# Places for the experts' weights: a ring of 15 in place of 5, and the blocks in another order

## The chip, the cores and the metric

The kernel runs on one core of one Trainium2 chip. The metric is the device time of one execution in microseconds (us). The kernel before took 3222.83 us as the median of three runs (3220.64 to 3227.54).

## What is computed

Three layers run one after the other over 512 tokens of 1024 features, all in float32. The change touches the mixture of experts in the second. There are 16 experts in 4 groups of 4; a token picks one group, and in it two experts:

```python
scores = jax.nn.sigmoid((t @ w_router).astype(jnp.float32))
sel = (scores + router_bias).reshape(-1, N_GROUPS, EXPERTS_PER_GROUP)
g_idx = jnp.argmax(lax.top_k(sel, TOP_K)[0].sum(-1), axis=-1)
in_group = jnp.take_along_axis(sel, g_idx[:, None, None], axis=1)[:, 0]
_, e_local = lax.top_k(in_group, TOP_K)
...
h = jax.nn.silu(jnp.einsum('td,edf->tef', t, w_gate)) * jnp.einsum('td,edf->tef', t, w_up)
y = jnp.einsum('tef,efd->td', h * combine[..., None], w_down)
```

Each expert's gate and up weights are 1024x256 and its down weights 256x1024. A layer norm (`ln1`) stands ahead of the experts, another (`ln2`) behind them.

## The kernel before

Each engine has its own program, written out by hand (`pe_experts`, `act_experts`, `dve_experts`, `pool_experts`), and they meet at semaphores. All weights lie in HBM as slabs of 128x1024 float32 (512 KB). SP, the queue of SyncE, loads them in order of use. The slab number n goes to place n % RING of a ring in SBUF, RING being 5, and its load waits until PE has used slab n - RING, which was there before it.

A float32 product is made of three products of rounded parts. For each slab, ACT copies a rounded high part to one of 3 buffers (`act_hi`), DVE subtracts it from the slab and writes the low part in place over the slab (`dve_lo`), and PE multiplies with both. ACT and DVE prepare slab i + 2 while PE uses slab i (`act_next`, `dve_next`: i + len(run.hi) - 1), since the high buffer of slab i + 3 is free only once PE is done with slab i.

**The experts.** The tokens are sorted into blocks of 128 rows: blocks 0 to 3 hold the first 128 tokens of groups 0 to 3, and three overflow blocks hold what is over 128 in any group. A block takes 24 slabs: 4 for the gate and up weights of each of its 4 experts (`up`), then 8 for the down weights (`down`). The seven blocks take 168 slabs, and go through in order: blocks 0 to 3 (96 slabs, loaded by SP), then the overflow blocks (72 slabs). Which group's weights an overflow block needs is known only from the router's result, so POOL loads those slabs with indirect DMAs (line 3488), whose row numbers lie in `m.place`. These too wait for slab n - RING.

In a block, PE does `up` for expert e, then `turn` (two transposes) for expert e - 1, and `rows` (8 small matmuls) once. The tokens of two blocks are brought to their rows at a time, by matmuls with one-hot matrices (`placed(g)`, 64 matmuls; `hot(g)` makes the matrices on DVE), ahead of `down` in blocks 1, 3 and 5. ACT and DVE copy the results to `m.xs`. Between the slabs ACT does the silu (`e_silu`) and copies the turned result (`e_Hhi`), and DVE does `gated` and `turned`. At a block's end ACT and DVE copy half of the output each (`m.ysb`), and ACT issues the store to `yd` (line 3298). At the very end POOL gathers each token's row from `yd` (line 3494).

`m.xs` and the one-hot matrices `m.hot` are each held twice, for the present pair of blocks and the next. In the last block DVE also adds 4 tiles of 128x1024 (`m.h`, the residual).

**Ahead of the experts** stands the stage `branches`. Its last slab on PE is used at 2344 us. ACT prepares the first experts' slabs in `act_first(K, m.we)`, as many as there are high buffers, ahead of `act_lnorm` for `ln1` (a table load, 8 squares, and the root); DVE takes two of them ahead of its last sum and the rest in `dve_first` behind its centring. PE sums the squares. Then come the router, transposes of the tokens (`x_trh`, `x_trl`), and `placed(0)`.

Line 410 is DVE's (and POOL's) tensor_tensor, line 403 ACT's copy, line 478 PE's matmul, line 482 its transpose.

```python
def act_hi(K, run, i):
    ...
    if i >= len(run.hi):
        A.wait_ge(*K.book.at("slab", run.name, i - len(run.hi)))
    elif run.behind:
        A.wait_ge(*K.book.at(*run.behind[i]))
    A.copy(run.hi[i % len(run.hi)][:, 0:run.offs[i][1]], raw, "hi", run.name, i)
```

Of the kernel before, what the change touches and what calls it, by code (L numbers as in the profile page):

```python
# [13 lines left out]
RING = 5  # L14
U32 = mybir.dt.uint32
SLAB = 1024
# [554 lines left out]


def landed(K, n):
    return K.book.at("slot%d" % (n % RING), n)


def raw_of(K, run, i):
    n = slab_at(K, "slab", run.name, i)
    size = run.offs[i][1]
    return n, K.ring[:, n % RING * SLAB:n % RING * SLAB + size], K.ring_r[n % RING][:, 0:size]  # L580

# [1468 lines left out]
def memory2(K, x):  # L2050
# [38 lines left out]
    m.xh = m.O[:, 0:8 * T]  # L2089
    m.xt, m.xs, m.hot, m.ysb = M(8 * T), M(16 * T), M(4 * T), [M(1024) for _ in range(2)]  # L2090
    m.xt_r, m.xl_r = M.rounded(m.xt, 1024), M.rounded(m.h, 1024)
# [3 lines left out]
    m.esg = [m.O[:, 8 * T + 256 * i:8 * T + 256 * i + 256] for i in range(4)]  # L2095
    wh = [M(1024), M(1024), m.O[:, 10 * T:12 * T]]
    m.x_r, m.xh_r = M.rounded(x, T), M.rounded(m.xh, T)
    m.we = Run(K, "experts", run_of(w0 + 89 * SLAB, 96) + [(None, SLAB)] * 72, wh, [("b_sum", 23)] * 3)
    m.wrh, m.wrl = M.rounded(M(256), 128)
# [5 lines left out]
    m.sw = [M(4) for _ in range(2)]  # L2105
    s = m.slot = M(292)
    m.slots = {"number": s[:, 0:256], "first": s[:, 256:272], "over": s[:, 272:288], "row": s[:, 288:289]}
# [1008 lines left out]

BLOCKS, PAIRS, EQ = 7, 4, ALU.is_equal


def pe_experts(K, m):  # L3120
# [39 lines left out]
    def placed(g):  # L3160

        P.wait_ge(*at("e_hot", g))
        P.wait_ge(*at("x_tl", 1, 3))
        for k in range(8):
            b = P.bank(1, "e_xs", g, k)
            for n, xt in enumerate((m.xt_r, m.xl_r)):
                for j in range(4):
                    P.mm(bk(b)[:, 256 * n:256 * n + 256], xt[j][:, 128 * k:128 * k + 128], m.hot_r[4 * (g % 2) + j][:], j == 0, j == 3)
            P.did("e_xsum", g, k)

    def rows(b):
        P.wait_ge(*at("r_w4"))
        o, S = P.bank(1, "e_rows", b), slice(128 * (b % 2), 128 * (b % 2) + 128)
        for n, w in enumerate((m.w4h, m.w4l)):
            for j in range(4):
                P.mm(bk(o)[:, 0:4], m.hot_r[4 * (b // 2 % 2) + j][:, S], w[:, 4 * j:4 * j + 4], n == 0 and j == 0, n == 1 and j == 3)
        P.did("e_rowed", b)

    def weights(i):
        n, raw = P.slab(m.we.offs[i][0], "slab", "experts", i)  # L3180
        P.wait_ge(*at("lo", "experts", i))
        return m.we.hi[i % 3], K.ring_r[n % RING]

    def up(b, e):
        o, lo = P.bank(1, "e_gated", b, e), 128 * (b % 2)
        for q in range(4):
            i = 24 * b + 4 * e + q
            wh, wl = weights(i)
            for h in range(2):
                k, C = 2 * q + h, slice(512 * h, 512 * h + 512)  # L3190
                xs = m.xs_r[8 * (b // 2 % 2) + k]
                P.wait_ge(*at("e_xs", b // 2, k))
                P.mm3([bk(o)], xs[:, lo:lo + 128], xs[:, 256 + lo:384 + lo], wh[:, C], wl[:, C], k == 0, k == 7)
            P.did("slab", "experts", i)
# [54 lines left out]
def act_experts(K, m, yd):  # L3249
# [16 lines left out]
    def placed(g, ks):  # L3266
        for k in ks:
            A.wait_ge(*at("e_xsum", g, k))
            A.copy(m.xs_r[8 * (g % 2) + k][:], out_of(K, 1, T, "e_xs", g, k), "e_xs", g, k)

# [5 lines left out]
    for b in range(BLOCKS):  # L3276
# [20 lines left out]
        A.wait_ge(*at("e_y", b, 1))  # L3297
        A.ready().dma_start(yd[128 * b:128 * b + 128, :], m.ysb[b % 2]).then_inc(*K.book.up("yst%d" % (b % 2), ("e_st", b), by=16))
    A.tables(ACT.Ln)
# [10 lines left out]
def dve_experts(K, m):  # L3310
# [14 lines left out]
    def hot(g):  # L3325
        for j in range(4):
            V.ts(m.hot_r[4 * (g % 2) + j][:], m.slots["number"], pos[:, j:j + 1], -256.0 * g, SUB, EQ, *(("e_hot", g) if j == 3 else ()))

# [11 lines left out]
    dve_shares(K, m)  # L3340
    hot(1)
    for b in range(BLOCKS):
        i = 24 * b
        for e in range(4):
            for q in range(4):
                dve_next(K, m.we, i)
                i += 1
            if e == 0:
                V.apart().wait_ge(*at("e_rowed", b))
                V.apart().cp(m.sw[b % 2], out_of(K, 1, 4, "e_rows", b), "e_rows", b)  # L3350
            gated(b, e)
            if e:
                turned(b, e - 1)
            if b == BLOCKS - 1:
                S = slice(1024 * e, 1024 * e + 1024)
                V.tt(m.h[:, S], m.xl_r[e][:], m.xt_r[e][:], ADD)
        if b % 2 and b // 2 + 1 < PAIRS:
            g = b // 2 + 1
            for k in range(1, 8, 2):
                V.wait_ge(*at("e_xsum", g, k))  # L3360
                V.cp(m.xs_r[8 * (g % 2) + k][:], out_of(K, 1, T, "e_xs", g, k), "e_xs", g, k)
            if g + 1 < PAIRS:
                hot(g + 1)
        for kk in range(8):
# [112 lines left out]
def pool_experts(K, m, table, wall, slots, yd):  # L3477
# [4 lines left out]
    G.wait_ge(*at("r_place"))  # L3482
    by_row = wall.rearrange("p (s c) -> (p s) c", c=SLAB)
    for n, (off, size, done) in enumerate(K.P.slabs):
        if off is None:
            slot = n % RING
            G.wait_ge(*at(*K.P.slabs[n - RING][2]))
            G.ready().indirect_dma_start(K.ring[:, slot * SLAB:slot * SLAB + SLAB], None, by_row,  # L3488
                                     bass.IndirectOffsetOnAxis(ap=m.place[:, 4 + (done[2] - 96) // 24:5 + (done[2] - 96) // 24], axis=0),
                                     element_offset=(done[2] - 96) % 24 * SLAB).then_inc(*K.book.up("gslot%d" % slot, ("slot%d" % slot, n), by=16))  # L3490
    for b in range(BLOCKS):
# [664 lines left out]
def layout_engines(nc, book, xT, out, con, par, wall, slots, at, blocks=(1, 2, 3)):  # L4156
# [11 lines left out]
    K.ring_r = K.mem.rounded(ring[:, :], SLAB)  # L4168
    half = K.mem.rounded(ring[:, :], HALF)
    K.halves = [half[2 * n:2 * n + 2] for n in range(RING)]  # L4170
    K.c, K.p = {}, {}
# [27 lines left out]
    with nc.Block() as block:  # L4199
# [63 lines left out]
        def _(eng):  # L4263
# [68 lines left out]
```

## Time and profile before

| | |
|---|---|
| median of 3 runs | 3222.83 us |
| the profiled execution's own time | 3222.16 us |
| its span, first to last instruction | 3220.1 us |
| PE busy | 2928.7 us (91%) |
| DVE busy | 1568.6 us (49%) |
| ACT busy | 1215.3 us (38%) |
| POOL busy | 826.5 us (26%) |
| moved by DMA | 283.09 MB, 88 GB/s over the span |
| issues of 512 KB by SP | 202, 3.7 us to landing |
| indirect DMAs of POOL | 72 |
| mean granted TensorE clock | 0.935 of full speed |

The page cuts the span into 40 slices of 80.5 us. Slices 31 to 34, from 2415 us to 2737 us, show 257, 275, 248 and 230 GB/s, where most others show 30 to 110. They lie within the experts' stage, and are the place to look at. The busy time of PE is modelled and takes in the overlap of matmuls, so the room on PE is better read from the starts of its weight loads (PEld).

### The profile page before, as it was taken

To read this page: it belongs to the slowest core of one execution; us is meant where nothing else is said; L and a number is where in the kernel's file an instruction comes from. 1 tells how busy PE (TensorE), PEld (TensorE's weight loads), DVE (VectorE), ACT (ScalarE), POOL (GpSimd) and SP (SyncE) were. 2 spreads that over 40 slices of the span, in tenths; PEclk is the share of its full clock that TensorE was granted. 3 is DMA by queue.
4 is the path that set the end of the run, shared out by engine and by line. 5 is a ranking of instruction groups with operands and counts; after the bars stand their busy time and mean duration, and the time that the engine had idled before them with its cause. 6 is when DMAs were issued, how large, how long until landed. Compare 5 with 4: busy or idle time off the path is not lost.

```text
span 3220.1 us, 54157 instructions
## 1 busy us (share of the span) xinstructions
PE 2928.7 (91%) x22694; PEld 2317.3 (72%) x22694; DVE 1568.6 (49%) x2880; ACT 1215.3 (38%) x2134; POOL 826.5 (26%) x814
## 2 busy tenths in 40 slices
PE   7899999999889999999899899998978887898998
PEld 6788888888767878887577677777756655556566
DVE  3544555455424344342443454566667766542433
ACT  2333333333322243232433344543255655442341
POOL 4222222222122100000345243541000055523243
PEclk9899899989889999999899898999999999878999
DMA  3111111111033333332122122224327877411112
GB/s 130 37 32 41 32 41 35 41 31 38 28 111 109 102 99 96 94 97 77 43 65 70 47 69 63 82 66 151 98 81 257 275 248 230 148 38 53 36 56 69
DMA packets 101266, 283.09 MB, mean 88 GB/s; under 512 B 11392, under 2 KB 11392, under 8 KB 99744
## 3 DMA queue, kind: packets, MB, share of 16 engines
q1 hardware_dynamic: 81968, 209.11, 21.5%
q0 software_dynamic: 14592, 60.56, 5.6%
q10 hardware_dynamic: 4464, 9.96, 0.8%
q8 instruction: 179, 2.93, 0.4%
q14 instruction: 63, 0.52, 0.1%
HBM read 261.24 MB, written 18.35 MB: 87 GB/s over the span
## 4 chain that ended last, share of the span: by engine, by line
PE 74%; DVE 10%; ACT 8%; DMA 5%; issue 2%; POOL 1%; ACTq 0%; DVEq 0%; SPq 0%; POOLq 0%
PE psum L478 72%; DVE arena L410 5%; ACT arena L395 4%; DMA ring<-in_w 3%; ACT arena L403 3%; DMA ring<-in_w,arena_whole 2%; PE psum L482 2%; DVE arena L419 2%; DVE ring L410 2%; ACT L390 1%; POOL ring L3488 1%; DVE arena L414 1%; DVE arena L422 1%; DVE arena L434 0%; DMA arena<-in_x 0%
## 5 line engine op out<-in xcount | busy, mean ns | idle before, releaser
L478 PE MATMUL psum<-arena,ring 128*128 128x512 f32 (+3 forms) x6152 | 1442.6, 365 | 13.5 <-DVE arena L410 6.9
L478 PEld LDWEIGHTS psum<-arena,ring 128*128 128x128 f32 (+2 forms) x6152 | 1024.4, 193 | 209.0 <-issue 35.6
L478 PE MATMUL psum<-arena 32*32 32x32 f32 (+16 forms) x12460 | 880.4, 254 | 154.2 <-DVE arena L410 58.4
L478 PE MATMUL psum<-arena,arena 128*128 128x512 f32 (+1 forms) x2896 | 887.4, 391 | 93.3 <-DVE ring L410 68.1
L478 PEld LDWEIGHTS psum<-arena 32*32 32x32 f32 (+10 forms) x12460 | 626.0, 142 | 360.9 <-issue 147.0
L478 PEld LDWEIGHTS psum<-arena,arena 128*128 128x128 f32 x2896 | 525.4, 190 | 257.5 <-DVE ring L410 108.5
L422 POOL CAST ring<-ring 128x512 fp32r<-128x512 f32 x332 | 231.3, 697 | 1370.9 <-DMA ring<-in_w 1248.5
L403 ACT ACTIVATE arena<-psum 128x512 f32<-128x512 f32 (+16 forms) x676 | 290.8, 448 | 746.9 <-PE psum L478 572.5
L410 DVE TENSOR_TENSOR ring<-ring,arena 128x1024 fp32r<-128x1024 f32 (+1 forms) x298 | 352.6, 1183 | 310.5 <-ACT arena L403 305.9
L403 ACT ACTIVATE arena<-ring 128x1024 fp32r<-128x1024 f32 (+1 forms) x298 | 305.6, 1026 | 500.2 <-PE psum L478 334.5
L410 POOL TENSOR_TENSOR ring<-ring,ring 128x512 fp32r<-128x512 f32 x332 | 440.2, 1326 | 26.7
L410 DVE TENSOR_TENSOR arena<-arena 128x528 f32<-128x528 f32 (+8 forms) x681 | 344.5, 519 | 205.0 <-ACT arena L395 115.4
L395 ACT ACTIVATE arena<-arena 128x512 f32<-128x512 f32 (+8 forms) x494 | 286.7, 587 | 325.4 <-DVE arena L410 167.6
L419 DVE SCALAR_TENSOR_TENSOR arena<-arena 128x512 f32<-128x512 f32 (+9 forms) x244 | 168.4, 691 | 235.3 <-ACT arena L395 230.4
L410 DVE TENSOR_TENSOR arena<-arena,psum 88x192 f32<-88x192 f32 (+4 forms) x276 | 112.3, 420 | 324.5 <-PE psum L478 321.0
L395 ACT ACTIVATE arena<-psum,arena 128x528 f32<-128x528 f32 (+8 forms) x206 | 115.1, 565 | 223.9 <-DVE arena L431 118.2
L3488 POOL DMA_INDIRECT ring<-in_w,arena_whole x72 | 89.1, 1237 | 292.9 <-PE psum L478 284.4
L482 PE MATMUL psum<-arena 128*128 128x128 f32 (+3 forms) x749 | 117.8, 288 | 23.1 <-DVE arena L410 9.6
L410 DVE TENSOR_TENSOR arena<-psum,arena 88x264 f32<-88x264 f32 (+3 forms) x177 | 81.9, 500 | 108.6 <-PE psum L478 60.0
L478 PE MATMUL psum<-ring,arena 128*128 128x512 f32 x336 | 133.6, 398 | 0.0
L419 DVE SCALAR_TENSOR_TENSOR arena<-psum,arena 128x512 f32<-128x512 f32 (+2 forms) x89 | 54.8, 629 | 150.7 <-PE psum L478 135.1
L390 ACT ACT_TABLE_LOAD x96 | 123.2, 1283 | 7.6 <-DVE arena L410 2.7
(50 smaller groups left out, 862.2 us busy)
## 6 DMA issues: line engine op xcount, KB each, us to landing
ring<-in_w SPq DMA_DIRECT2D x202, 512.0 KB, 3.7
ring<-in_w SPq DMA_DIRECT2D x356, 256.0 KB, 2.7
bg<-arena ACTq DMA_DIRECT2D x24, 256.0 KB, 2.3
yd<-arena ACTq DMA_DIRECT2D x7, 512.0 KB, 6.4
arena<-bg POOLq DMA_DIRECT2D x1, 3072.0 KB, 17.0
arena<-in_x SPq DMA_DIRECT2D x1, 2112.0 KB, 15.0
od<-arena POOLq DMA_DIRECT2D x8, 256.0 KB, 2.4
oy<-arena POOLq DMA_DIRECT2D x8, 256.0 KB, 3.0
```

The lines of the kernel that those rows point to most:

```text
L390: self.eng.preload_act_table_set(name)
L395: self.own(self.ready().activation(out, a, f, bias=bias, scale=scale, accum_out=accum), event)
L403: self.own(self.ready().activation(out, a, ACT.Copy, scale=scale), event)
L410: self.own(self.ready().tensor_tensor(out, a, b, op), event)
L414: self.own(self.ready().tensor_scalar(out, a, s1, None, op0), event)
L419: self.own(self.ready().scalar_tensor_tensor(out=out, in0=a, scalar=s, in1=b, op0=op0, op1=op1), event)
L422: self.own(self.ready().tensor_copy(out, a), event)
L478: self.last_ins = self.eng.matmul(out, l, r, start=start, stop=stop, skip_group_check=skip)
L482: self.last_ins = self.eng.transpose(out, a, self.ident[0:n, 0:n])
L3488: G.ready().indirect_dma_start(K.ring[:, slot * SLAB:slot * SLAB + SLAB], None, by_row, bass.IndirectOffsetOnAxis(ap=m.place[:, 4 + (done[ ...
```

## The change

- The experts' slabs get 15 places: the 5 of the ring, 4 (`m.soon`) that come free when the stage `branches` has ended on PE, ACT and DVE, and 6 (`m.late`) that come free when the tokens' last transpose is done (`x_trl`). A slab's load waits for the use of the slab that had its place before, 15 back within the experts (`slot_of`, `emptied_by`).
- The high buffers become 5, so ACT and DVE work 4 slabs ahead of PE.
- The room comes from `m.xs` and `m.hot`, which are now held once. `hot(1)` leaves the place ahead of the first block; `hot(g + 1)` stands in block 1, 3 and 5, behind DVE's first four slabs.
- The order of blocks is `TURNS`: groups 0 and 1, overflow 4 and 5, groups 2 and 3, overflow 6. Rows of `yd` and numbers of positions follow it.
- What is computed, and the number of matmuls, slabs and DMAs, stay.

```diff
+def slot_of(K, n):
+    first = K.book.now.get(("slab", "slab", "experts", 0))
+    if first is not None and first <= n < first + len(K.m2.we.offs):
+        i = (n - first) % len(K.raw)
+        return (first + i) % RING if i < RING else i
+    return n % RING
+
+
+def emptied_by(K, slabs):
+
+    last, out = {}, []
+    for n in range(len(slabs)):
+        out.append(last.get(slot_of(K, n)))
+        last[slot_of(K, n)] = n
+    return out
...
-    return n, K.ring[:, n % RING * SLAB:n % RING * SLAB + size], K.ring_r[n % RING][:, 0:size]
+    return n, K.raw[slot_of(K, n)][:, 0:size], K.ring_r[slot_of(K, n)][:, 0:size]
...
-    m.xt, m.xs, m.hot, m.ysb = M(8 * T), M(16 * T), M(4 * T), [M(1024) for _ in range(2)]
+    m.xt, m.xs, free, m.hot, m.ysb = M(8 * T), M(8 * T), [M(SLAB) for _ in range(5)], M(2 * T), [M(1024) for _ in range(2)]
...
-    wh = [M(1024), M(1024), m.O[:, 10 * T:12 * T]]
+    wh = [M(1024), M(1024), m.O[:, 10 * T:12 * T]] + free[:2]
...
-    m.we = Run(K, "experts", run_of(w0 + 89 * SLAB, 96) + [(None, SLAB)] * 72, wh, [("b_sum", 23)] * 3)
+    m.we = Run(K, "experts", [q for b in TURNS for q in (run_of(w0 + (89 + 24 * b) * SLAB, 24) if b < 4 else [(None, SLAB)] * 24)], wh, [("b_sum", 23)] * 5)
...
+    m.soon = free[2:] + [M(SLAB)]
+    m.late = [x[:, SLAB * i:SLAB * i + SLAB] for i in range(4)] + [m.O[:, 2 * T:4 * T], m.O[:, 6 * T:8 * T]]
...
+TURNS = (0, 1, 4, 5, 2, 3, 6)
...
-        return m.we.hi[i % 3], K.ring_r[n % RING]
+        return m.we.hi[i % len(m.we.hi)], K.ring_r[slot_of(K, n)]
...
-                xs = m.xs_r[8 * (b // 2 % 2) + k]
+                xs = m.xs_r[k]
...
-            A.copy(m.xs_r[8 * (g % 2) + k][:], out_of(K, 1, T, "e_xs", g, k), "e_xs", g, k)
+            A.copy(m.xs_r[k][:], out_of(K, 1, T, "e_xs", g, k), "e_xs", g, k)
...
-        A.ready().dma_start(yd[128 * b:128 * b + 128, :], m.ysb[b % 2]).then_inc(*K.book.up("yst%d" % (b % 2), ("e_st", b), by=16))
+        A.ready().dma_start(yd[128 * TURNS[b]:128 * TURNS[b] + 128, :], m.ysb[b % 2]).then_inc(*K.book.up("yst%d" % (b % 2), ("e_st", b), by=16))
...
-            V.ts(m.hot_r[4 * (g % 2) + j][:], m.slots["number"], pos[:, j:j + 1], -256.0 * g, SUB, EQ, *(("e_hot", g) if j == 3 else ()))
+            V.ts(m.hot_r[j][:], m.slots["number"], pos[:, j:j + 1], -128.0 * TURNS[2 * g], SUB, EQ, *(("e_hot", g) if j == 3 else ()))
...
     hot(0)
     dve_shares(K, m)
-    hot(1)
     for b in range(BLOCKS):
...
                 V.apart().cp(m.sw[b % 2], out_of(K, 1, 4, "e_rows", b), "e_rows", b)
+                if b % 2 and b // 2 + 1 < PAIRS:
+                    hot(b // 2 + 1)
...
-            if g + 1 < PAIRS:
-                hot(g + 1)
...
+    before = emptied_by(K, K.P.slabs)
     for n, (off, size, done) in enumerate(K.P.slabs):
         if off is None:
-            slot = n % RING
-            G.wait_ge(*at(*K.P.slabs[n - RING][2]))
+            slot = slot_of(K, n)
+            G.wait_ge(*at(*K.P.slabs[before[n]][2]))
...
+    K.m2 = m2
+    K.raw += m2.soon + m2.late
+    K.ring_r += [K.mem.rounded(q, SLAB)[0] for q in m2.soon + m2.late]
...
             for n, (off, size, done) in enumerate(slabs):
-                if n >= RING and off is not None:
-                    sp.wait_ge(*book.at(*slabs[n - RING][2]))
                 if off is None:
                     continue
-                slot = n % RING
-                eng.dma_start(ring[:, slot * SLAB:slot * SLAB + size], wall[:, off:off + size]).then_inc(*book.up("slot%d" % slot, ("slot%d" % slot, n), by=16))
+                slot = slot_of(K, n)
+                if before[n] is not None:
+                    sp.wait_ge(*book.at(*slabs[before[n]][2]))
+                elif slot >= RING + len(m2.soon):
+                    sp.wait_ge(*book.at("x_trl", 1, 3))
+                elif slot >= RING:
+                    for e in ("pe", "act", "dve"):
+                        sp.wait_ge(*book.at("end", e, "branches"))
+                eng.dma_start(K.raw[slot][:, 0:size], wall[:, off:off + size]).then_inc(*book.up("slot%d" % slot, ("slot%d" % slot, n), by=16))
```


## Rows read from the trace of the kernel before

**Rows 1.** Waits, 2395 to 2755 us: engine, line, waited for, us, times, longest.
```profile
PEld psum L478 <- DVE ring L410: 96.7, 98, 2.7
...
ACT arena L403 <- DMA ring<-in_w,arena_whole: 56.6, 49, 3.1
ACT arena L403 <- DMA ring<-in_w: 44.4, 51, 3.1
```

**Rows 2.** The chain that ended last, by line, 2395 to 2752 us.
```profile
by line: PE psum L478 27.7%; DMA ring<-in_w 17.8%; DMA ring<-in_w,arena_whole 16.8%; DVE ring L410 12.3%; ACT arena L403 8.4%; POOL ring L3488 6.3%; issue 5.2%; DVE arena L410 1.5%; DVE arena L419 1.2%; DVE arena L422 1.0%; DVE arena L416 0
```

**Rows 3.** Timeline of PE: the stage's first and last expert matmuls (start, us, instruction, count).
```profile
2395.43 0.39 PE L478 MATMUL psum<-ring,arena 128*128 128x512 f32 x1
...
2751.34 0.40 PE L478 MATMUL psum<-arena,arena 128*128 128x512 f32 x1
```

**Rows 4.** Timeline of PEld: a turn, a slab, the rows, a placement.
```profile
2408.73 0.37 PEld L482 LDWEIGHTS psum<-arena 128*128 128x128 f32 x2
...
2427.96 0.19 PEld L478 LDWEIGHTS psum<-ring,arena 128*128 128x128 f32 x1
...
2429.35 0.19 PEld L478 LDWEIGHTS psum<-ring,arena 128*128 128x128 f32 x1
...
2448.04 1.43 PEld L478 LDWEIGHTS psum<-arena,arena 128*128 128x128 f32 x10
...
2568.32 7.86 PEld L478 LDWEIGHTS psum<-arena,arena 128*128 128x128 f32 x65
```

**Rows 5.** Timeline of DVE in blocks 0 and 1.
```profile
2409.15 1.23 DVE L410 TENSOR_TENSOR ring<-ring,arena 128x1024 fp32r<-128x1024 f32 x1 [0.48 <-ACT arena L403]
2410.41 0.48 DVE L419 SCALAR_TENSOR_TENSOR arena<-arena,psum 128x256 f32<-128x256 f32 x1
2410.93 0.42 DVE L410 TENSOR_TENSOR arena<-psum,arena 128x256 fp32r<-128x256 f32 x1
...
2440.46 0.68 DVE L422 COPY arena<-psum 128x512 f32<-128x512 f32 x1
2442.76 1.23 DVE L410 TENSOR_TENSOR ring<-ring,arena 128x1024 fp32r<-128x1024 f32 x1 [1.62 <-ACT arena L403]
```

**Rows 6.** Windows: us, busy of PE, PEld, DVE, ACT, POOL, then PEclk, DMA share, GB/s.
```profile
2544.00:2547.00 3.00, 3.00 (x19) 2.59 (x18) 1.23 (x1) 0.16 (x1) 0.00 (x0) 1.00 1.02 404
...
2400.00:2570.00 170.00, 146.41 (x649) 108.78 (x648) 124.08 (x130) 105.09 (x124) 0.00 (x0) 0.99 0.84 275
2583.00:2743.00 160.00, 126.98 (x544) 92.51 (x543) 107.16 (x108) 86.83 (x101) 88.71 (x72) 0.98 0.76 243
```

**Rows 7.** POOL's indirect DMAs: all of line 3488, then timelines.
```profile
L3488 POOL DMA_INDIRECT ring<-in_w,arena_whole x72: 932/1140/1984, 2583.9 to 2742.4; - x72
...
DMA to landing us min/median/max: 4.2/5.5/7.9
...
2688.31 1.43 POOL L3488 DMA_INDIRECT ring<-in_w,arena_whole  x1 [0.30 <-issue]
...
2760.28 0.93 POOL L3494 DMA_INDIRECT arena<-yd,arena_whole  x1 [0.31 <-issue]
```

**Rows 8.** Ahead of the stage: SP's landings, then timelines of SP, ACT, PE, DVE.
```profile
DMA to landing us min/median/max: 2.5/3.4/5.8
...
2344.35 0.33 SPq L4278 DMA_DIRECT2D ring<-in_w  x1
...
2336.11 1.28 ACT L390 ACT_TABLE_LOAD   x1
2347.13 1.23 ACT L395 ACTIVATE arena<-arena 128x512 f32<-128x512 f32 x2 [9.74 <-DVE arena L419]
...
2351.34 9.20 PE L478 MATMUL psum<-arena 128*128 128x512 f32 x16 [5.04 <-ACT arena L395]
...
2346.41 4.88 DVE L419 SCALAR_TENSOR_TENSOR arena<-psum,arena 128x512 f32<-128x512 f32 x8 [1.29 <-PE psum L478]
...
2381.91 2.82 PE L482 MATMUL psum<-arena 128*128 128x128 f32 x24
```

More of the change, by code:

```diff
@@ L570, in slab_at @@
     return K.book.get(("slab",) + done, 0)
+def slot_of(K, n):
[10 more added lines that the diff above has]
+    return out
 def landed(K, n):
-    return K.book.at("slot%d" % (n % RING), n)
+    return K.book.at("slot%d" % slot_of(K, n), n)
 def raw_of(K, run, i):
@@ L2105, in memory2 @@
     m.sw = [M(4) for _ in range(2)]
-    s = m.slot = M(292)
+    s = m.slot = M(296)[:, 0:292]
+    m.soon = free[2:] + [M(SLAB)]
+    m.late = [x[:, SLAB * i:SLAB * i + SLAB] for i in range(4)] + [m.O[:, 2 * T:4 * T], m.O[:, 6 * T:8 * T]]
     m.slots = {"number": s[:, 0:256], "first": s[:, 256:272], "over": s[:, 272:288], "row": s[:, 288:289]}
@@ L3167, in placed @@
                 for j in range(4):
-                    P.mm(bk(b)[:, 256 * n:256 * n + 256], xt[j][:, 128 * k:128 * k + 128], m.hot_r[4 * (g % 2) + j][:], j == 0, j == 3)
+                    P.mm(bk(b)[:, 256 * n:256 * n + 256], xt[j][:, 128 * k:128 * k + 128], m.hot_r[j][:], j == 0, j == 3)
             P.did("e_xsum", g, k)
@@ L3175, in rows @@
             for j in range(4):
-                P.mm(bk(o)[:, 0:4], m.hot_r[4 * (b // 2 % 2) + j][:, S], w[:, 4 * j:4 * j + 4], n == 0 and j == 0, n == 1 and j == 3)
+                P.mm(bk(o)[:, 0:4], m.hot_r[j][:, S], w[:, 4 * j:4 * j + 4], n == 0 and j == 0, n == 1 and j == 3)
         P.did("e_rowed", b)
@@ L3360, in dve_experts @@
                 V.wait_ge(*at("e_xsum", g, k))
-                V.cp(m.xs_r[8 * (g % 2) + k][:], out_of(K, 1, T, "e_xs", g, k), "e_xs", g, k)
-            if g + 1 < PAIRS:
-                hot(g + 1)
+                V.cp(m.xs_r[k][:], out_of(K, 1, T, "e_xs", g, k), "e_xs", g, k)
         for kk in range(8):
@@ L3483, in pool_experts @@
     by_row = wall.rearrange("p (s c) -> (p s) c", c=SLAB)
+    before = emptied_by(K, K.P.slabs)
     for n, (off, size, done) in enumerate(K.P.slabs):
         if off is None:
-            slot = n % RING
-            G.wait_ge(*at(*K.P.slabs[n - RING][2]))
-            G.ready().indirect_dma_start(K.ring[:, slot * SLAB:slot * SLAB + SLAB], None, by_row,
-                                     bass.IndirectOffsetOnAxis(ap=m.place[:, 4 + (done[2] - 96) // 24:5 + (done[2] - 96) // 24], axis=0),
-                                     element_offset=(done[2] - 96) % 24 * SLAB).then_inc(*K.book.up("gslot%d" % slot, ("slot%d" % slot, n), by=16))
+            slot = slot_of(K, n)
+            G.wait_ge(*at(*K.P.slabs[before[n]][2]))
+            G.ready().indirect_dma_start(K.raw[slot], None, by_row,
+                                     bass.IndirectOffsetOnAxis(ap=m.place[:, TURNS[done[2] // 24]:TURNS[done[2] // 24] + 1], axis=0),
+                                     element_offset=done[2] % 24 * SLAB).then_inc(*K.book.up("gslot%d" % slot, ("slot%d" % slot, n), by=16))
     for b in range(BLOCKS):
@@ L4169, in layout_engines @@
     half = K.mem.rounded(ring[:, :], HALF)
+    K.raw = [ring[:, n * SLAB:n * SLAB + SLAB] for n in range(RING)]
     K.halves = [half[2 * n:2 * n + 2] for n in range(RING)]
@@ L4271, in _ @@
             slabs = K.P.slabs
+            before = emptied_by(K, slabs)
             for n, (off, size, done) in enumerate(slabs):
-                if n >= RING and off is not None:
-                    sp.wait_ge(*book.at(*slabs[n - RING][2]))
                 if off is None:
                     continue
-                slot = n % RING
-                eng.dma_start(ring[:, slot * SLAB:slot * SLAB + size], wall[:, off:off + size]).then_inc(*book.up("slot%d" % slot, ("slot%d" % slot, n), by=16))
+                slot = slot_of(K, n)
[7 more added lines that the diff above has]
+                eng.dma_start(K.raw[slot][:, 0:size], wall[:, off:off + size]).then_inc(*book.up("slot%d" % slot, ("slot%d" % slot, n), by=16))
                 if slabs[n][2] == ("slab", "gates", 27):
```

## The prediction

> **What bounds the kernel now.** I went from the page's slices (which stretch moves most bytes) to the waits of that stretch, then to the chain, then to timelines of single slabs. In the experts' stage PE waits 96.7 us in 98 pieces for DVE's low parts, and behind them ACT waits 44.4 and 56.6 us for the slabs to land [rows 1]. The chain says the same: 17.8% and 16.8% of it are landings, 6.3% POOL's issues, only 27.7% PE [rows 2]. So the loop is: PE frees a place, the load is issued and lands, ACT and DVE prepare, PE uses. With 5 places and 3 high buffers that loop is longer than the slabs that cover it. The stage goes from 2395.4 to 2751.7 us, 356.3 us for 168 slabs, 2.12 us each [rows 3].
>
> **What PE needs if nothing is late.** Weight loads of low parts of the same slab position stand 1.39 us apart where nothing waits (2427.96 to 2429.35) [rows 4]: 168 x 1.39 = 233.5 us. A turn takes 0.37: 28 x 0.37 = 10.4. The eight matmuls of `rows` lie in ten loads of 1.43 us, of which two are the slab's: 1.0 each, 7.0 in all. A placement is 7.86 us, three of them inside the stage: 23.6 [rows 4]. The sum is 274.5 us, 82 below today. A block without a placement is 33.4 + 1.5 + 1.0 = 35.9 us.
>
> **Part 1, 15 places.** A load may now be issued up to 15 slabs ahead. A slab's landing takes 4.2 to 7.9 us by POOL's row [rows 7], its preparation 1.06 on ACT and 1.23 on DVE; 10 slabs that lie ready ahead of ACT are 15 us of PE's work, so latency is covered. What is left is rate. A slab is 0.524 MB. The stage moves 275 and 243 GB/s with the DMA engines busy 0.84 and 0.76, and 404 GB/s at full share in 2544 to 2547 [rows 6]. The bounds are 275/0.84 = 327 GB/s, 1.60 us a slab, and 404, 1.30 us. The first 15 slabs land ahead of the stage (below); 153 x 1.60 = 245 us is less than 274.5, so even the slow bound hides, and the stretches at 1.49 us a slab live off the full places. Cost on the path: nothing, as long as PE takes 1.6 us a slab on average.
>
> **Part 2, the 15 at the start.** The ring's five land as today, the last issued at 2344.35 [rows 8]. The four `soon` loads wait for the stage's end, the root just behind PE's sums (2351.34 + 9.20 = 2360.5), so about 2362. The six `late` ones wait for the transposes, 2381.91 + 2.82 = 2384.7: six at 1.3 to 1.6 us and 3.4 us of latency end at 2396 to 2398, and the first is needed at 9 x 1.39 behind the start less 5 slabs ahead, 2401. Behind SP's new waits stand only slabs that nobody needs earlier.
>
> **Part 3, five high buffers.** `act_first` now also prepares slabs 3 and 4, and stands in ACT's program ahead of the table load and squares of `ln1`. Slab 4 is issued at 2344.35, lands at 3.4 us, 2347.8; copy 1.06, table load 1.28, and the first square is done at about 2350.8, where today the squares begin at 2347.13. But PE starts its sums at 2351.34 at any rate: DVE's centring ends at 2346.41 + 4.88 = 2351.29, and the sum's bank is the one that it reads [rows 8]. PE takes longer over a sum than ACT over a square, so this costs 0; with the longest landing, 5.8 us, it would cost 2. The two further low parts on DVE lie in its idle time behind the centring. `hot(1)` leaves the start and goes to block 1; it delayed only DVE's fourth slab.
>
> **Part 4, DVE, the next late one.** A low part takes 1.26 us start to start, `gated` 0.52, `turned` 0.46, the output copy 0.7 [rows 5]. A block: 24 x 1.26 + 4 x 0.98 + 0.9 = 35.0 us. Behind the output copy DVE waits 1.62 us for ACT [rows 5], whose store waits for that copy and whose next high part stands behind the store. So 36.7 us on DVE against 35.9 on PE. The 4 slabs of lead (5.6 us) cover this in one block; in the block with a placement DVE has 1.5 (hot) + 2.8 us more and PE 7.86, and the lead is restored. I count 1 us of PE stall a pair, 3 us. In the last block DVE has 4 x 1.26 = 5.0 us more for the residual: 4 us of stall. Sum 7, bounds 0 (all covered) and 17 (DVE bound all the way).
>
> **Part 5, the order of blocks and POOL.** POOL's issue takes 88.71/72 = 1.23 us on average [rows 6], up to 1.98, and 0.93 where DVE is nearly idle, with 0.30 between two [rows 7]: 1.53, between 1.24 and 2.28 a slab. It can begin on slab 48 when slab 33 is used. The slab 44 further on must have landed when PE is through slab 87: 54 x 1.49 + 7.9 = 88.4 us. 44 pitches and 5.5 us of landing fit if the pitch is below 1.88. I take 1.75, since DVE will be busier and the mean must rise; it hides. In one row of 72 the lead would be spent; with two groups loaded by SP between, it is refilled. In the last block there are 23 pitches and a landing in 33 x 1.49 + 7.9 = 57.1 us, 2.24 each.
>
> The Trainium skill speaks against this part. "SBUF — State Buffer", section "Who interferes with whom", says that a VectorE instruction with two inputs in SBUF contends with a GpSimd instruction that reads SBUF, and infers that making descriptors is not touched. By the first half the pitch would near its slow bound, and the time be that of the POOL rival below, 3164 us; by the second it would stay at its mean, and the time at the forecast. The spread 0.93 to 1.98 speaks for some contention.
>
> **The sum.** Stage 274.5 + 7 = 281.5, against 356.3: 75 us less. The profiled execution took 3222.16 us, 2.1 more than its span and within 0.7 of the median of the three runs, so the result is 3222 - 75 = 3147 us. Behind the stage nothing changes but that block 3's first two slabs may be loaded a little earlier.
>
> **Rivals.**
> - *DVE and ACT bound all the way* (14%). Every block takes 36.7, the odd ones wait for the placement and add their copies: 7 x 36.7 + 3 x 10 (placement 7.9, hot 1.5, a last copy) + 5 = 292 us, 3157 us. For it: DVE's sum is above PE's. Against: the placements give PE's time back to DVE three times.
> - *POOL's issue bound* (10%). At 2.28 us a slab, 44 x 2.28 + 5.5 = 105.8 against 88.4: 17 us, 3164 us. Today a busy DVE already stretches the issues, and POOL has 6.3% of the chain [rows 2].
> - *The DMA engines are at their rate* (6%). If deeper queues move no more than today's 275 and 243 GB/s, 81 slabs of 1.91 and 72 of 2.16 us are 310 us, with 5 for the last: 315, so 3181 us. Against: the share was not full, and 404 GB/s was seen.
> - *Slower* (3%). POOL is starved of its turns by a DVE that never pauses. The 44 and 23 pitches p of part 5 stand against 88.4 and 57.1 us less 11 of landing: PE's stall is 67 p - 134.5. It eats the gain of 75 at p = 3.13 us. If each issue waits for two whole low parts more, 0.93 + 2 x 1.26 + 0.30 = 3.75 us, the stall is 117 us and the time 3264. Against it: the longest of 72 is 1.98, and when PE stalls DVE pauses too.
> - *The change doesn't do what it says* (2%): a place is free later than I read, and the lead stays at five. Then it is 3222.
>
> **How the numbers follow.** The forecast of 3147 has 65%. Its own bounds are 274.5 us of stage (3140) and a little from the earlier slabs of block 3 at the low end, 3137; the high end takes in the DVE and POOL rivals and a late square, and some of the way to the DMA one: 3170. Left out are the rest of that rival and the two below. A measurement of this kernel can tell 0.2% from no change. Faster by more than that 95%, within it 2%, slower 3%.
>
> **What would show it.** Right: PE's wait for DVE's low parts falls from 96.7 to under 20 us; ACT's waits for landings go to nearly nothing in the blocks of SP and of POOL; DVE is over 90% busy in the stage; the stage ends near 2677 us; POOL's waits for PE are short and its issues 1.3 to 1.6 us long; the granted clock stays near today's 0.98 to 0.99 [rows 6]. PE's sums for `ln1` still start near 2351.3. Wrong: ACT waits for indirect slabs in block 3 of the new order (POOL), waits for landings everywhere at a DMA share near 1 (rate), or PE waits for DVE evenly over all blocks (DVE).

## The result

The changed kernel takes 3149.15 us (median of four runs, 3143.32 to 3149.49), the kernel before in the same sessions 3225.18 us (3220.64 to 3229.49). The ratio is 0.976, with a 95% interval of 0.9741 to 0.9779. The forecast of 3147 us was 2 us off. The profiled execution has a span of 3141.2 us, against 3220.1 before.

All of it comes from the experts' stage, and the profile shows where.

Timeline of PE in the changed kernel, the stage's first and last expert matmuls (start, us, instruction, count), against [rows 3]:

```profile
2396.36 0.39 PE L478 MATMUL psum<-ring,arena 128*128 128x512 f32 x1
...
2672.26 0.40 PE L478 MATMUL psum<-arena,arena 128*128 128x512 f32 x1
```

The stage takes 276.2 us from 2396.4 to 2672.6, where it took 356.2: 80 us less. What lies behind it takes 468.6 us in the one and 468.4 in the other. What lies ahead of it is 0.9 us longer in this execution, 0.7 of which was there before the change touches anything.

The waits in that stage (engine, line, waited for, us, times, longest), against [rows 1]:

```profile
POOL ring L3509 <- PE psum L478: 94.4, 7, 85.2
POOL arena L3509 <- PE psum L478: 89.8, 9, 79.4
ACT arena L403 <- PE psum L478: 43.5, 91, 1.3
...
DVE arena L410 <- ACT arena L403: 11.1, 15, 1.9
PEld psum L478 <- DVE arena L410: 5.6, 8, 1.5
...
DVE ring L410 <- ACT arena L403: 4.3, 4, 1.6
...
PEld psum L478 <- DVE ring L410: 0.5, 1, 0.5
```

PE's wait for low parts fell from 96.7 to 6.1 us. ACT's two rows of waits for landings (44.4 and 56.6 us) are gone; no row has them. ACT now waits for PE, that is, for a free high buffer, which is where a prepared slab should wait.

Windows (us, busy of PE, PEld, DVE, ACT, POOL, then PEclk, DMA share, GB/s), against [rows 6]:

```profile
2396.00:2448.00 52.00, 51.70 (x240) 42.35 (x239) 45.77 (x55) 41.44 (x48) 0.48 (x1) 1.00 0.92 340
2448.00:2526.00 78.00, 76.97 (x381) 63.79 (x380) 70.50 (x75) 59.31 (x69) 55.30 (x48) 1.00 0.89 325
2526.00:2605.00 79.00, 77.77 (x384) 64.50 (x383) 71.21 (x77) 60.27 (x70) 0.16 (x1) 1.00 0.91 339
...
2396.00:2672.00 276.00, 270.05 (x1313) 222.80 (x1312) 248.86 (x272) 205.07 (x239) 84.34 (x72) 1.00 0.83 306
```

The second window holds the indirect slabs of two blocks, the third those of SP. Both move 325 and 339 GB/s at a share of 0.89 and 0.91, where it was 243 and 275 at 0.76 and 0.84. DVE is busy 249 of 276 us. The granted clock is at its upper level, 2.4 GHz, all through the stage. Before, windows of 4 us show it down in three places: 0.57 of full speed at 2444, 0.74 and 0.84 at 2596 and 2600, 0.64 and 0.94 at 2648 and 2652. If that is a part of each window at 1.2 GHz and the rest at 2.4, it makes some 3.4 us at the lower level in each of the three (an estimate).

The chain of the stage by line, against [rows 2]:

```profile
by line: PE psum L478 35.2%; DVE arena L410 32.7%; DVE ring L410 14.2%; issue 5.1%; ACT arena L403 3.8%; DVE arena L419 3.0%; DVE arena L416 1.6%; DVE arena L422 1.6%; DMA yd<-arena 1.1%; DVE arena L425 0.7%; PE psum L482 0.6%; ACTq L3319 0
```

No transfer of weights is left in it. PE has 35.2% and DVE's low parts 32.7 and 14.2%: the two now run nearly level, as part 4 of the prediction had it. "Issue" (5.1%) is time that the profile gives to no releaser.

### The profile page after: what moved, and what is told of

It reads as the page before. It is cut to its first block, busy times and chain, and to the rows that moved or that the text cites. A ratio compares the mean times of both kernels' runs of the same rounds, so it can differ in the third digit from the quotient of the medians.

```text
span 3141.2 us, 54158 instructions
## 1 busy us (share of the span) xinstructions
PE 2902.8 (92%) x22694; PEld 2322.3 (74%) x22694; DVE 1571.5 (50%) x2880; ACT 1216.4 (39%) x2134; POOL 820.5 (26%) x814
## 4 chain that ended last, share of the span: by engine, by line
PE 75%; DVE 14%; ACT 7%; DMA 2%; issue 2%; ACTq 0%; POOL 0%; SPq 0%; DVEq 0%; POOLq 0%
PE psum L478 74%; DVE arena L410 7%; ACT arena L395 4%; ACT arena L403 2%; DVE arena L419 2%; PE psum L482 2%; DVE ring L410 1%; DMA ring<-in_w 1%; ACT L390 1%; DVE arena L414 1%; DVE arena L422 1%; DVE arena L434 0%; DMA arena<-in_x 0%; DVE arena L416 0%; DVE arena L438 0%
## 5 line engine op out<-in xcount | busy, mean ns | idle before, releaser
L478 PE MATMUL psum<-arena,arena 128*128 128x512 f32 (+2 forms) x3116 | 879.0, 387 | 36.2 <-DVE arena L410 15.8
L478 PEld LDWEIGHTS psum<-arena,arena 128*128 128x128 f32 (+1 forms) x3116 | 563.6, 189 | 175.3 <-issue 25.7
L403 ACT ACTIVATE arena<-ring 128x1024 fp32r<-128x1024 f32 (+1 forms) x188 | 189.2, 1006 | 394.0 <-PE psum L478 325.0
L410 DVE TENSOR_TENSOR ring<-ring,arena 128x1024 fp32r<-128x1024 f32 (+1 forms) x188 | 217.6, 1157 | 222.6 <-ACT arena L403 218.7
L403 ACT ACTIVATE arena<-arena 128x1024 fp32r<-128x1024 f32 (+5 forms) x274 | 191.7, 707 | 67.7 <-DVE arena L410 27.2
L410 DVE TENSOR_TENSOR arena<-arena,arena 128x1024 fp32r<-128x1024 f32 (+4 forms) x196 | 203.6, 1039 | 18.6 <-ACT arena L403 11.8
L482 PEld LDWEIGHTS psum<-arena 128*128 128x128 f32 (+3 forms) x749 | 90.5, 141 | 48.0 <-DVE arena L419 10.4
```

The lines of the kernel that those rows point to most:

```text
L403: self.own(self.ready().activation(out, a, ACT.Copy, scale=scale), event)
L410: self.own(self.ready().tensor_tensor(out, a, b, op), event)
L478: self.last_ins = self.eng.matmul(out, l, r, start=start, stop=stop, skip_group_check=skip)
L482: self.last_ins = self.eng.transpose(out, a, self.ident[0:n, 0:n])
```

## The experiments

The time of a whole execution drifts by 5 us and more from one to the next. In the profiled executions the drift lies on both sides of the stage: its first matmul stands between 2395 and 2412 us, and what lies behind it takes 465.4 to 472.9 us, though the code there is the same in most. The length of the stage itself repeats to 0.1 us in the four kernels of 15 places whose difference does not touch it (276.19 to 276.25). How well it repeats where landings bound it is not known: each of those kernels has one profile. So what tells the kernels apart is the stage, from its first expert matmul to the first matmul behind it:

| kernel | places | high buffers | order | stage, us | median, us | ratio to before, 95% interval |
|---|---|---|---|---|---|---|
| before | 5 | 3 | old | 356.2 | 3222 to 3227 | |
| e5_order_alone | 5 | 3 | new | 350.6 | 3227.1 | 1.0007 (0.9989 to 1.0025) |
| e3_five_places | 5 | 5 | new | 367.1 | 3242.8 | 1.0054 (1.0031 to 1.0078) |
| e6_seven_places | 7 | 5 | new | 297.9 | 3178.4 | 0.9869 (0.9835 to 0.9903) |
| e4_nine_places | 9 | 5 | new | 278.9 | 3151.7 | 0.9789 (0.9766 to 0.9812) |
| e2_three_high | 15 | 3 | new | 307.7 | 3186.8 | 0.9887 (0.9864 to 0.9910) |
| e1_old_order | 15 | 5 | old | 276.2 | 3147.6 | 0.9764 (0.9738 to 0.9791) |
| the change | 15 | 5 | new | 276.2 | 3149.2 | 0.9760 (0.9741 to 0.9779) |
| p1_slow_pool | 15 | 5 | new | 298.4 | 3170.8 | 0.9833 (0.9806 to 0.9860) |
| p2_slow_pool_old_order | 15 | 5 | old | 301.3 | 3171.5 | 0.9836 (0.9805 to 0.9867) |
| g1_other_bank | 15 | 5 | new | 276.2 | 3150.3, one run | |
| g2_bank_and_high | 15 | 5 | new | 276.2 | 3147.8 | 0.9748 (0.9721 to 0.9774) |
| h1_adds_earlier | 15 | 5 | new | 276.1 | 3156.5 | 0.9788 (0.9751 to 0.9825) |
| h2_best | 15 | 5 | new | 276.0 | 3144.0 | 0.9757 (0.9728 to 0.9785) |

The rival theories were three: the places carry the gain, the lead of ACT and DVE carries it, or the order of the blocks does. Each of these was undone alone.

### The order of the blocks

```diff
-TURNS = (0, 1, 4, 5, 2, 3, 6)
+TURNS = (0, 1, 2, 3, 4, 5, 6)
```

> The changed kernel with one part undone: the blocks go through in the old order (0 to 6), so all 72 slabs of POOL come in one row. Theory: POOL's issues stand 1.48 us apart in the changed kernel where they follow one another, and PE takes 1.49 us a slab without the placements, so POOL never falls behind and the order is worth nothing: stage 276 us as in the changed kernel (2396.4 to 2672.5), time 3149 within 3 us, no wait of ACT for an indirect slab. Rival: the lead of 15 is spent in the long row and the order was needed: ACT waits for indirect slabs in blocks 5 and 6, the stage grows by 5 to 17 us, 3154 to 3166 us.

The stage is 276.24 us against 276.23, and ACT waits for no landing. With 15 places the order is worth nothing.

Is it an insurance against a slow POOL? Two memsets ahead of each indirect DMA give the price:

```diff
+    m.scrap = M(256)
...
+            for _ in range(2):
+                G.ms(m.scrap, 0.0)
             G.ready().indirect_dma_start(K.raw[slot], None, by_row,
```

> The changed kernel with two memsets of 128x256 on POOL ahead of each of its 72 indirect DMAs, some 0.65 us more an issue, 1.48 to about 2.1 us from issue to issue. It prices the lead of 15 against a slow issuer. Theory: PE is through slab 87 at 54 x 1.49 + 7.9 = 88.4 us behind slab 33, and 44 issues of 2.1 us with 6.2 us of landing are 98.6: the stage grows by 5 to 14 us, seen as waits of ACT for indirect slabs in the blocks just ahead of groups 2 and 3, and by under 2 us in the last block. Rival: issues are not what counts with 15 places, and the stage stays at 276 to 279 us.

> As the run before it (two memsets of 128x256 ahead of each indirect DMA), but with the blocks in the old order, 72 indirect slabs in one row. Theory: the order is an insurance: 71 issues of 2.1 us and 6.2 of landing are 155 us against 81 x 1.49 + 15.8 = 136.5, so 15 to 24 us more of stage than 276, and 5 to 13 us more than with the new order. Rival: the order is worth nothing here either, both within 2 us.

The issues were stretched more than meant: over the first 48 they stand 2.33 us apart in both kernels (2451.6 to 2561.1 in the new order). With that figure the prediction's sum gives 44 x 2.33 + 6.2 - 88.4 = 20 us of stall in the new order and 71 x 2.28 + 6.2 - 136.5 = 32 in the old (2.28 being the mean spacing over all 72 there, 2530.1 to 2691.9). Measured are 22.2 and 25.1 us. So the lead is spent in both orders. The sum holds for the new order and is 7 us too high for the old one, and why is open. The new order saves 3 us where 5 to 13 were expected, and the medians, 3170.8 and 3171.5 us, do not tell the two apart. The waits are where they should be in the slowed kernel of the new order, in the blocks ahead of groups 2 and 3 (first two rows) and none in the stretch behind, where PE waits 0.3 us, for a gated product (last row). In the last block ACT waits 7.7 us for landings, but PE's waits for DVE there are 3.4 us against 3.3 in the changed kernel:

```profile
ACT arena L403 <- DMA arena<-in_w,arena_whole: 13.1, 11, 1.7
...
ACT arena L403 <- DMA ring<-in_w,arena_whole: 5.1, 3, 4.0
...
PE psum L482 <- DVE arena L419: 0.3, 1, 0.3
```

### The places

```diff
-    m.soon = free[2:] + [M(SLAB)]
+    m.soon = []
...
-    m.late = [x[:, SLAB * i:SLAB * i + SLAB] for i in range(4)] + [m.O[:, 2 * T:4 * T], m.O[:, 6 * T:8 * T]]
+    m.late = []
```

This is the kernel of five places; that of nine empties only `m.late`; that of seven empties `m.late` and cuts `m.soon` to `free[2:4]`.

> The changed kernel with 5 places (no further ones) but 5 high buffers and the new order. Theory (the places carry most): the loop of a place, landing 4.6 to 6, high 1.1, low 1.3, PE 1.4 and the waits in the order of ACT and DVE, stays, so PE's wait for DVE stays over 60 us and ACT waits for landings over 70: stage 330 to 356 us, time 3203 to 3229. Rival (the lead of ACT and DVE was the bound): stage under 310 us, time under 3183.

> The changed kernel with 9 places (the 5 and the 4 of m.soon, not the 6 of m.late). Theory (latency is what was to be covered): 9 places are 9 x 1.49 = 13.4 us of PE's work against a loop of 8.6 to 10.6 us, so nearly all of the gain is there: stage 276 to 284 us, time 3149 to 3157. Rival (it is the spread of landings and POOL's issues, or the rate, that needs the deep ring): stage over 292 us, time over 3165.

> The changed kernel with 7 places (the ring and 2 of m.soon). Five places with this lead took 367 us for the stage, nine 279. Theory (a loop of latency over places): the loop of 10 to 11 us is spread over 7 places, 1.5 us a slab, just what PE takes, so the stage is 285 to 305 us: time 3158 to 3178. Rival (a smooth line between 5 and 9, set by rate): near 323 us, time 3196.

Nine places give 77.3 of the 80 us, seven 58.3, and five with the lead of four none. The gain stops between 7 x 1.49 = 10.4 and 9 x 1.49 = 13.4 us of PE's work, as a loop of latency would have it, and seven places are far from the 323 us of a smooth line. The loop is not one constant, though: 367.1 us over 168 slabs and five places make 10.9 us, 297.9 over seven make 12.4 (estimates from the table). The rate of transfer, a rival with 6% in the forecast, did not bind: the nine places move 312 GB/s over the stage, where that rival had 243 and 275.

But five places with five high buffers came out slower than either theory, 367 us and above the kernel before. Either the new order or the longer lead costs there. Taking the lead away as well tells them apart:

```diff
-    wh = [M(1024), M(1024), m.O[:, 10 * T:12 * T]] + free[:2]
+    wh = [M(1024), M(1024), m.O[:, 10 * T:12 * T]]
```

The number of conditions in `m.we` goes from 5 back to 3 with it.

> The changed kernel with 5 places and 3 high buffers: of the change only the new order of blocks and the single copies of m.xs and m.hot are left. It is to tell why 5 places with 5 high buffers took 367 us for the stage, 11 more than the kernel before. Theory: the lead of 4 did it, since ACT's high part of slab i + 3 stands ahead of the silu in its program and now waits for a slab whose place PE has only just freed; then this kernel is as the one before, stage 352 to 360 us, time 3222 within 5 us. Rival: the order (or the single copies) costs with a short ring; then the stage stays at 363 us or more, time over 3229.

The stage falls to 350.6 us, 5.6 below the kernel before and a little below the 352 to 360 of the theory. So the lead of four cost 16.5 us with a short ring. In this one profile the order, or the single copies, gave 5.6 us; between those two no run decides. The whole kernel does not bear the 5.6 us out: its ratio to the kernel before is 1.0007, and the lower end of its interval is a gain of 3.5 us. Waits of five places with five high buffers, then with three:

```profile
DVE ring L410 <- ACT arena L403: 111.4, 84, 5.6
...
ACT arena L403 <- DMA ring<-in_w: 70.2, 61, 4.5
ACT arena L403 <- DMA ring<-in_w,arena_whole: 67.3, 56, 5.7
```

```profile
DVE ring L410 <- ACT arena L403: 81.6, 92, 2.7
...
ACT arena L403 <- DMA ring<-in_w,arena_whole: 51.3, 48, 3.1
ACT arena L403 <- DMA ring<-in_w: 44.5, 55, 2.5
```

With the longer lead ACT waits 137.5 us for landings, with the shorter 95.8. ACT's program has the high part of slab i + 3 ahead of the silu that PE's slab i - 1 has set free. When the place of slab i + 3 was itself freed just now, the silu stands behind a landing. That this is the path follows from the program's order and fits the rows; no run moved the silu.

### The high buffers

> The changed kernel with 15 places but 3 high buffers, so that ACT and DVE work 2 slabs ahead. Theory (both parts are needed): behind each expert's fourth slab PE finds the next low part 0.5 us late (silu 0.4, turned 0.4, high 1.1, low 1.3 against 2 x 1.39), 28 times, and behind each output copy some 2 us late, six times: stage 276 + 26 = 302 us, time 3175. Rival (the places alone carry the gain): the stage stays under 280 us, time 3149 to 3153.

The edit is that of the three high buffers just above, alone. The stage is 307.7 us, 5.7 over the theory's 302, and the time 3186.8 us, 12 over its 3175. Both parts are needed, as it says: 15 places without the lead leave 31.5 of the 80 us on the table. The waits moved, as expected, from landings to the chain of ACT and DVE:

```profile
ACT arena L403 <- PE psum L478: 75.8, 98, 3.1
PEld psum L478 <- DVE arena L410: 28.4, 35, 2.2
DVE arena L410 <- ACT arena L403: 25.2, 43, 1.9
PE psum L478 <- DVE arena L410: 17.1, 20, 1.8
```

### What covered the two high parts ahead of ln1

The prediction put the cost of the two further high parts at nothing, since PE's sums waited for a bank of PSUM anyway. Giving the sums another bank, alone and with the two high parts moved, tests it:

```diff
+    K.P.nbank += 1
     pe_sum8(K, "ln1", m.O, T2)
...
-    act_first(K, m.we)
-    act_lnorm(K, "ln1", m.h, m.O, m.rs, T)
+    for _ in range(3):
+        act_more(K, m.we)
+    A.tables(ACT.Ln)
+    act_squares(K, "ln1", m.h, m.O, T, [("centred", "ln1", k) for k in range(8)])
+    act_first(K, m.we)
+    act_root(K, "ln1", m.rs, T, 1.0 / 1024, K.c["eps5"])
```

> The changed kernel with the sums for ln1 in another bank, and the fourth and fifth high part left ahead of the squares. Theory: the bank covered them by only a few tenths, so without that cover the squares' start (2351.0) bounds the sums: they begin 0.3 to 0.5 us earlier than now, 6.7 to 6.9 us behind the last sum of the stage before, where now it is 7.2 and was 3.7 with both edits. Rival: the bank alone was the wait, and it is 3.7 us here too.

> The changed kernel with PE's sums for ln1 in another bank than the one that DVE's centring still reads, and with ACT's fourth and fifth high part moved from ahead of the squares to between the squares and the root. Theory: what covered those two high parts was that the sums waited for that bank until 2352.05; with both moved, squares begin with the centring (some 3 us earlier than 2351.0) and the sums start 2.5 to 3.5 us earlier, the experts' first matmul too, stage unchanged at 276: time 3 us lower. Rival: the sums wait for something else (the squares' own order), and nothing moves, within 0.5 us.

Timelines of PE, last sums of the stage before and the sums of the squares: the change, the other bank alone, and both edits:

```profile
2344.88 2.14 PE L478 MATMUL psum<-arena 128*128 128x512 f32 x4
2352.05 9.44 PE L478 MATMUL psum<-arena 128*128 128x512 f32 x16 [5.04 <-DVE arena L419]
```

```profile
2348.24 2.14 PE L478 MATMUL psum<-arena 128*128 128x512 f32 x4
2355.07 9.71 PE L478 MATMUL psum<-arena 128*128 128x512 f32 x16 [4.69 <-ACT arena L395]
```

```profile
2352.48 2.14 PE L478 MATMUL psum<-arena 128*128 128x512 f32 x4
2356.13 7.13 PE L478 MATMUL psum<-arena 128*128 128x512 f32 x16 [1.51 <-ACT arena L395]
```

The distance between the two rows is 7.17 us in the changed kernel and was 7.18 before the change (2344.16 and 2351.34 there): the high parts cost nothing. With the other bank alone it is 6.83, so the cover was 0.34 us deep. With both edits it is 3.65. The sums themselves take 7.13 instead of 9.44 us. The windows show what goes with it: ahead of them PE pauses 1.51 us instead of 5.04, and the clock granted over them is 1.00 of full speed (2.4 GHz throughout) instead of 0.76, with part of them at 1.2 GHz. With the other bank alone the pause is 4.69 us, the clock 0.74, and the sums take 9.71. The change, then both edits:

```profile
2352.00:2362.00 10.00, 9.44 (x16) 3.88 (x16) 3.68 (x3) 3.77 (x8) 0.78 (x2) 0.76 0.06 17
```

```profile
2356.00:2364.00 8.00, 7.13 (x16) 2.95 (x16) 7.27 (x10) 7.07 (x11) 1.01 (x2) 1.00 0.07 19
```

The way from the last sums to the experts' first matmul falls from 51.5 (2344.9 to 2396.4) to 47.2 us (2352.5 to 2399.6), 4.3 us. In the median, 3147.84 us against 3149.15 in other sessions, this is not to be told from the drift.

### DVE's additions in the last block

```diff
-            if b == BLOCKS - 1:
-                S = slice(1024 * e, 1024 * e + 1024)
-                V.tt(m.h[:, S], m.xl_r[e][:], m.xt_r[e][:], ADD)
...
+            if b == BLOCKS - 2 and kk in (0, 1, 3, 5):
+                j = (0, 1, 3, 5).index(kk)
+                S = slice(1024 * j, 1024 * j + 1024)
+                V.tt(m.h[:, S], m.xl_r[j][:], m.xt_r[j][:], ADD)
```

> The changed kernel with one edit: DVE's four residual additions (4 x 1.26 us) taken out of the last block and put among the last eight slabs of the block before it, whose placement has let DVE catch up. My prediction gave them 4 us of PE stall. Theory: PE's wait for DVE in the last block (2.1 us for low parts and 1.2 for a gated product) falls to under 1 us, stage 274 to 275 us. Rival: they only come out as stall one block earlier, stage 276 us.

> The changed kernel with three edits that the runs so far point to: the sums for ln1 in another bank, two high parts moved behind the squares (the run with both gained 4.3 us from the last slab of the stage before to the first expert matmul), and DVE's four residual additions taken out of the last block and put among the last eight slabs of the one before it. Theory: 4.3 us at the start and up to 2 us in the last block, stage 274 to 276 us, time 4 to 6 us below the changed kernel. Rival: the additions are not what PE waits for in the last block, stage 276.2, only the 4.3 us.

The stage is 276.1 and 276.0 us. The theory's 274 to 275 us missed and the rival holds. The median of the edit alone, 3156.5 us, is 7 above the changed kernel's; in the profiled execution the stage is no longer, but begins at 2407.9 instead of 2396.4 us. In the last block PE's rows of waits for low parts fall from 2.1 to 0.2 us, but as much comes back where the two blocks meet. Weight loads of the kernel with this edit alone, then its DVE:

```profile
2648.73 3.72 PEld L478 LDWEIGHTS psum<-arena,arena 128*128 128x128 f32 x20 [1.19 <-issue]
2653.44 1.68 PEld L478 LDWEIGHTS psum<-arena,arena 128*128 128x128 f32 x8 [0.99 <-issue]
```

```profile
2641.16 8.78 DVE L410 TENSOR_TENSOR arena<-arena,arena 128x1024 fp32r<-128x1024 f32 x7
2649.86 0.68 DVE L422 COPY arena<-psum 128x512 f32<-128x512 f32 x1
2652.16 2.48 DVE L410 TENSOR_TENSOR arena<-arena,arena 128x1024 fp32r<-128x1024 f32 x2 [1.62 <-issue]
```

The two pauses of 1.19 and 0.99 us have no releaser in the profile, but they end 0.04 us behind the end of a low part (2641.16 + 6 x 1.255 = 2648.69, and 2652.16 + 1.25 = 2653.41), as PE's named waits for DVE do. So the 4 x 1.26 us only pass to the block before, as the rival says: DVE has no room in either. That DVE is what these pauses wait for is read from the times, since the profile names nothing.

The kernel with all three edits has the way of 47.2 us again and a median of 3143.96 us, ratio 0.9757 (0.9728 to 0.9785), against 0.9760 of the change. The profile shows 4.3 us gained, the intervals do not tell it from the change.

## Why the prediction was right, point by point

- **What bounds the kernel, and what PE needs.** Right. The floor of 274.5 us was some 4.4 too high: PE is busy 270.05 of the stage's 276 us (last window above). PE's timeline, below, shows which terms: a turn adds 0.22 us, not 0.37, and `rows` 0.90, not 1.0. That is 28 x 0.15 + 7 x 0.10 = 4.9 us. The 0.37 was the length of the turn's weight loads, part of which lies beside PE's matmuls.
- **15 places (part 1).** Right, and deeper than needed: nine give all but 2.7 us of it. The windows above have 339 GB/s at a share of 0.91, so 373 at full share, between the two bounds of 327 and 404.
- **The 15 at the start (part 2).** Right: PE waits for no slab at the beginning, and the first wait of PE for a low part in the stage is 0.3 us, at 2443.6.
- **Five high buffers (part 3).** Right, with the mechanism and almost the depth: the squares began at 2351.03 against 2350.2 as forecast, the sums were not moved, and 0.34 us of cover was left. What I read as cover was itself a stall: with another bank, and the high parts moved out of the squares' way, the sums come 3.5 us earlier.
- **DVE (part 4).** Right, in size too: 7 us of stall were forecast, PE's matmuls waited 5.9 us for DVE (4.1 for low parts and 1.8, in the turns, for gated products). 2.5 us of it lie ahead of the last block, against 3 for the three pairs, and 3.3 in it, against 4 for the residual.
- **The order and POOL (part 5).** The outcome was right, two steps in it were wrong. I expected issues of POOL to come further apart, 1.75 us, since DVE would be busier. They take 1.17 us each on average, against 1.24 before, with the 0.30 between two 1.47 against 1.54, and in the runs where they keep step with DVE they stand 1.26 apart. The sign of issues 1.3 to 1.6 us long did not come. And "in one row of 72 the lead would be spent" is refuted: the old order gives the same stage, and even at 2.33 us an issue the two orders differ by 3 us. My own sum would have said so, had I made it for the old order: (81 x 1.49 + 15.8 - 5.5)/71 = 1.85 us, where the new one has 1.88.
- **The sum.** 75 us forecast, 80 in the stage of the profiled executions, 76 in the medians. The stage was forecast 5.3 us too long, nearly all of it the floor. That the median hit so closely has luck in it: it lies 5.8 us above the profiled execution's time of 3143.32.

The two terms on PE in the changed kernel, `rows` first. A matmul of a slab starts 0.23 us behind the one before it. From 2401.21 to 2402.80 there are three of these (0.69) and the eight of `rows`, which leaves 0.90; from 2422.30 to 2422.97 there are two (0.46) and a turn, which leaves 0.21, and another turn gives 0.23:

```profile
2401.21 0.39 PE L478 MATMUL psum<-ring,arena 128*128 128x512 f32 x1
2401.44 1.51 PE L478 MATMUL psum<-arena,arena 128*128 128x512 f32 x10
2402.80 0.40 PE L478 MATMUL psum<-ring,arena 128*128 128x512 f32 x1
...
2422.30 0.39 PE L478 MATMUL psum<-arena,arena 128*128 128x512 f32 x1
2422.53 0.38 PE L482 MATMUL psum<-arena 128*128 128x128 f32 x2
2422.66 0.47 PE L478 MATMUL psum<-arena,arena 128*128 128x512 f32 x1
2422.97 0.39 PE L478 MATMUL psum<-ring,arena 128*128 128x512 f32 x1
```

Why POOL came out faster can be read from two timelines of the changed kernel, POOL's and then DVE's:

```profile
2478.01 1.90 POOL L3509 DMA_INDIRECT ring<-in_w,arena_whole  x1 [0.30 <-issue]
2480.22 0.96 POOL L3509 DMA_INDIRECT arena<-in_w,arena_whole  x1 [0.30 <-PE psum L478]
2481.48 0.95 POOL L3509 DMA_INDIRECT arena<-in_w,arena_whole  x1 [0.30 <-issue]
2482.74 0.95 POOL L3509 DMA_INDIRECT arena<-in_w,arena_whole  x1 [0.30 <-issue]
2483.99 1.54 POOL L3509 DMA_INDIRECT arena<-in_w,arena_whole  x1 [0.30 <-PE psum L478]
```

```profile
2477.88 5.00 DVE L410 TENSOR_TENSOR arena<-arena,arena 128x1024 fp32r<-128x1024 f32 x4 [1.62 <-ACT arena L403]
2482.80 0.15 DVE L422 COPY arena<-psum 128x4 f32<-128x4 f32 x1
2482.99 0.48 DVE L419 SCALAR_TENSOR_TENSOR arena<-arena,psum 128x256 f32<-128x256 f32 x1
2483.51 5.00 DVE L410 TENSOR_TENSOR arena<-arena,arena 128x1024 fp32r<-128x1024 f32 x4
```

DVE's low parts follow each other every 1.25 us, and POOL's issues fall into step with them, 1.26 apart and 0.95 long, each starting just ahead of the end of a low part. The issue at 2478.01 began 0.13 us behind the start of a low part and took 1.90.

Laying the two timelines side by side for all 72 issues of this kernel shows one rule. The 67 that begin while a low part runs take 0.94 us, and on top of it what is then left of that low part beyond 0.16 us; this holds within 0.07 us for each of them. At 2478.01 there was 1.12 us left, which gives 1.90; at 2483.99 it was 0.76, which gives 1.54, as measured. Four that begin while DVE is idle take 0.93 to 0.94. In the kernel before, the 18 that begin beside an idle DVE take 0.93 to 0.94 too, and so do the two that begin during a copy out of PSUM and two that begin at the same moment as a low part. So an issue waits for the rest of one low part, and not for the next. In the changed kernel 40 of the 67 begin with 0.2 us or less left; before it was 8 of 50. That is the step, and with it the mean is 1.17 us against 1.24. An undisturbed issue and the 0.30 behind it make 1.24 us, almost DVE's 1.25, so two engines that are once in step stay so. That this near equality is what keeps them in step is argued; no run changed DVE's spacing.

The Trainium skill ("SBUF — State Buffer", section "Who interferes with whom") has VectorE with two inputs in SBUF contend with a GpSimd instruction that reads SBUF, and infers that making descriptors is not touched. By the single rows the trace agrees with the first half, 1.90 against 0.95, and not with the inference. The time came out as by the second half all the same: the slow bound of 2.28 us, which I took from the longest issue and to which the first half would have led, did not come.

## What to carry to other kernels

Measure the loop from "place free" to "used" against (places) x (the bound engine's time a slab): the gain stops where the product passes the loop, here between seven and nine of the fifteen places. Add places before lead: an engine that works ahead in program order waits for a landing with everything behind it, and with five places a lead of four cost 16.5 us where it gave 31.5 with fifteen (both measured; the reason for the cost is argued from the program's order). When a whole kernel drifts by more than an edit is worth, compare the stretch between two instructions that the edit leaves in place.

## What the runs showed of the hardware that was not expected

- An indirect DMA issue of POOL takes 0.94 us and on top of it what is left of DVE's tensor_tensor of 128x1024 at its start beyond 0.16 us, up to 1.93 us; it never waits for a second one (67 of 67 issues within 0.07 us). Beside back-to-back tensor_tensors of 1.25 us the issues fall in step, 1.26 us apart, which is hardly slower than undisturbed.
- The DMA engines carry 512 KB slabs at 325 to 340 GB/s over stretches of 52 to 79 us with a share of about 0.9, from SP's queue and POOL's alike, where a ring of five had 243 to 275.
- Three dips of the granted clock in the stage (to 0.57, 0.74 and 0.64 of full speed in windows of 4 us) are gone in the kernel whose PE is idle for 6 of 276 us and not for 59 of 356, and the sums for ln1 run in 7.13 instead of 9.44 us where the pause ahead of them is 1.5 instead of 5.0 us.
